# Expert blocks of an encoder layer: token rows through slot tables in DRAM instead of gather and scatter matmuls

## The reference

```python
def swiglu(x, w_gate, w_up, w_down):
    return (jax.nn.silu(x @ w_gate) * (x @ w_up)) @ w_down

logits = (xt @ w_router).astype(F32)
top_val, top_idx = lax.top_k(logits, TOP_K)          # TOP_K = 2 of 8
top_w = jax.nn.softmax(top_val, axis=-1)
...                                                  # slots grouped by expert into 128-row blocks
yp = lax.map(run, (xp.reshape(n_blocks, MOE_BLOCK, D), block_e)).reshape(P, D)   # run = swiglu
contrib = yp[dest] * w_s[:, None].astype(x.dtype)
out = jnp.zeros((T, D), x.dtype).at[tok_s].add(contrib)
```

## Time and profile before

| | |
|---|---|
| median of 3 runs | 1494.04 us (1493.0 to 1494.84) |
| span of the profiled execution | 1493.8 us |
| mixer 0, dense feed-forward, mixer 1 | 0 to 640 us |
| last mixer slabs, router, start of block 0 | 640 to 697 us |
| eight expert blocks, 98.45 us each | 692 to 1482 us |
| last scatter, additions, store | 1482 to 1493.8 us |
| busy: PE, DVE, ACT | 96%, 79%, 59% |

### The profile page before, as it was taken

One profiled execution on the slowest core, in us unless ns is written; L12 is line 12 of the kernel. 1 busy time (PEld: TensorE's weight loads), 2 busy tenths in 40 slices (PEclk: granted clock), 3 DMA queues, 4 the chain that ended last, 5 costly groups with the idle time before them and its releaser, 6 DMA issues.

```text
span 1493.8 us, 19784 instructions
## 1 busy us (share of the span) xinstructions
PE 1435.4 (96%) x6848; PEld 1177.4 (79%) x6848; DVE 1184.9 (79%) x1249; ACT 878.6 (59%) x944; POOL 40.9 (3%) x53
## 2 busy tenths in 40 slices
PE   6999898999999999888999999999999999999997
PEld 4887677788878876677888888888888888888786
DVE  5989875554459897746988989989898798898986
ACT  4345644434334456434777767777677677776774
POOL 0020001000000110100000000000000000000000
PEclk9999999999999999996999999999999999999999
DMA  7443224755244342332989979989799799897993
GB/s 285 174 174 141 85 87 154 271 190 195 92 169 170 141 151 104 134 113 100 385 296 360 386 281 387 353 296 393 280 370 387 273 396 339 318 387 279 374 385 110
DMA packets 56673, 372.06 MB, mean 249 GB/s; under 512 B 6706, under 2 KB 7278, under 8 KB 16570
## 3 DMA queue, kind: packets, MB, share of 16 engines
q1 hardware_dynamic: 55914, 368.82, 65.7%
q0 software_dynamic: 720, 2.72, 0.6%
HBM read 370.47 MB, written 1.05 MB: 249 GB/s over the span
## 4 chain that ended last, share of the span: by engine, by line
PE 82%; DVE 10%; issue 5%; ACT 2%; DVEq 0%; POOL 0%; DMA 0%; SPq 0%; POOLq 0%; ACTq 0%
PE bank L1536 19%; PE bank L1286 18%; PE bank L1287 17%; PE bank L1513 11%; PE bank L1333 5%; DVE w_lo L846 4%; PE bank L1299 3%; PE bank L1558 2%; PE bank L1328 2%; PE bank L1436 2%; PE bank L1423 1%; DVE ys L835 1%; DVE x L1194 1%; PE bank L1416 1%; ACT w_hi L570 1%
## 5 line engine op out<-in xcount | busy, mean ns | idle before, releaser
L846 DVE TENSOR_TENSOR w_lo<-raw,w_hi 128x2048 fp32r<-128x2048 f32 (+2 forms) x382 | 802.4, 2108 | 141.7 <-ACT w_hi L570 133.8
L570 ACT ACTIVATE w_hi<-raw 128x2048 fp32r<-128x2048 f32 (+2 forms) x382 | 674.0, 1769 | 179.8 <-PE bank L1536 97.6
L1286 PE MATMUL bank<-w_hi,hT_hi 128*128 128x512 f32 (+1 forms) x1232 | 492.1, 399 | 3.3 <-DVE act L1157 1.6
L1287 PE MATMUL bank<-w_hi,hT_lo 128*128 128x512 f32 (+1 forms) x1232 | 478.9, 389 | 0.0
L1286 PEld LDWEIGHTS bank<-w_hi,hT_hi 128*128 128x128 f32 x1232 | 233.0, 189 | 52.5 <-issue 5.5
L1287 PEld LDWEIGHTS bank<-w_hi,hT_lo 128*128 128x128 f32 x1232 | 233.3, 189 | 43.5 <-issue 1.0
L1513 PE MATMUL bank<-w_lo,hT_hi 128*128 128x512 f32 (+1 forms) x880 | 231.2, 385 | 0.0
L1513 PEld LDWEIGHTS bank<-w_lo,hT_hi 128*128 128x128 f32 x880 | 164.6, 188 | 31.6 <-DVE w_lo L846 0.3
L749 ACT ACTIVATE act_hi<-bank 128x256 fp32r<-128x256 f32 (+1 forms) x99 | 40.4, 408 | 138.5 <-PE bank L1299 138.5
L1536 PE MATMUL bank<-w_hi,act_lo 128*128 128x512 f32 (+1 forms) x440 | 118.7, 392 | 1.8 <-DVE act_lo L1163 1.8
L1536 PE MATMUL bank<-w_hi,act_hi 128*128 128x512 f32 (+1 forms) x440 | 119.0, 393 | 0.8 <-ACT act_hi L749 0.8
(11 more groups left out here) (212 smaller groups left out, 1115.6 us busy)
## 6 DMA issues: line engine op xcount, KB each, us to landing
raw<-in_moe SPq DMA_DIRECT2D x224, 1024.0 KB, 7.0
raw<-in_mix SPq DMA_DIRECT2D x56, 1024.0 KB, 4.9
raw<-in_dense SPq DMA_DIRECT2D x28, 1024.0 KB, 4.8
raw<-in_moe SPq DMA_DIRECT2D x42, 512.0 KB, 3.5
raw<-in_moe SPq DMA_DIRECT2D x16, 768.0 KB, 5.9
raw<-in_dense SPq DMA_DIRECT2D x5, 512.0 KB, 3.3
raw<-in_moe SPq DMA_DIRECT2D x8, 256.0 KB, 3.4
raw<-in_dense SPq DMA_DIRECT2D x2, 768.0 KB, 4.3
```

Source lines behind the costliest of these rows:

```text
L570: nc.scalar.activation(HI[:, split_slot, 0:width], RAW[:, raw_slot, 0:width], ACT.Copy)\
L846: vec.tensor_tensor(LO[:, split_slot, 0:width], RAW[:, raw_slot, 0:width], HI[:, split_slot, 0:width].bitcast(F32), ALU.subtract).then_inc ...
L1286: mm(out_, left[0], right[0], start=start, stop=False)
L1287: mm(out_, left[1], right[1], start=False, stop=False)
```

## The change

Two tables in DRAM are added, `slot_h` and `slot_y`, of 13 slots of 128 rows of 1024 floats. `slot_h` and the last four slots of `slot_y` are filled with zeros early in layer 0's feed-forward part, by two DMAs that ACT issues from a zeroed piece of `x_squared`. The router computes for each token and each of its two experts a row number (`rowi`), and POOL writes the normalized rows of all tokens to `slot_h` by four indirect DMAs of 128 rows. ACT loads the 128 rows of block 0 to `tok`; for all later blocks SP loads them, in the middle of the block before. PE transposes `tok` with eight transposes instead of the gather's 32 matmuls, ACT copies the result to `hT_hi`, and DVE subtracts for `hT_lo`. On the way back ACT and DVE each copy one bank of 512 columns to `y`, unscaled, and SP stores `y` to `slot_y` in the middle of the next block. After the last block POOL fetches each token's two result rows by four indirect DMAs, and DVE multiplies them with the token's weights and adds them to `x`. `psel`, `pselT`, `hg_hi`, `hg_lo`, `y_hi`, `y_lo` and all their matmuls and additions are gone. The order of the slabs is as before.

```diff
-    def router(dve, v, tt, ts, stt, gather_lo):
+    def router(dve, v, tt, ts, stt):
...
+        tt(place[:, :, :], counted, per_token(base), ALU.add)
+        ts(far[:, :, :], counted, float(CAP), None, ALU.is_ge, None, *drain_of(1, "pos", 0))
...
+        tt(chosen[:, 0, :, :], place[:, :, :], sel1[:, :, :], ALU.mult)
+        tt(chosen[:, 1, :, :], place[:, :, :], sel2[:, :, :], ALU.mult)
+        v.settle()
+        reduce(flat(R["rowf"][:, :, :]), chosen[:, :, :, :].rearrange("p k t e -> p (k t) e"))
+        v.settle()
+        v.do(vec.tensor_copy(R["rowi"][:, :, :], R["rowf"][:, :, :]), sem("rows_known"), 1)
...
@@ SP, block_slabs, between slabs 27 and 28
+                if b is not None:
+                    sp.wait_ge(tok_turned, 2 * b + 2)
+                    sp.dma_start(R["tok"][0:CAP, :], slot_h[bass.ds(sp.snap(CAP * b + 2 * CAP), CAP), :])\
+                        .then_inc(tok_loaded, 16)
+                    sp.wait_ge(y_taken, 2 * b + 2)
+                    sp.dma_start(slot_y[bass.ds(sp.snap(CAP * b), CAP), :], R["y"][0:CAP, :]).then_inc(y_free, 16)
...
@@ SP, the end
-        sp.wait_ge(scatter_added, 4 * nb + 4)
-        sp.dma_start(out.rearrange("(p t) d -> p t d", t=TB), X[:, :, :]).then_inc(sem("stored"), 16)
+        sp.wait_ge(y_taken, 2 * nb + 2)
+        sp.dma_start(slot_y[bass.ds(sp.snap(CAP * nb), CAP), :], R["y"][0:CAP, :]).then_inc(sem("last_y_stored"), 16)
+        out_rows = out.rearrange("(p t) d -> p t d", t=TB)
+        for tb in range(TB):
+            sp.wait_ge(sem("combined"), tb + 1)
+            sp.dma_start(out_rows[:, tb, :], X[:, tb, :]).then_inc(sem("stored"), 16)
...
@@ POOL
+        pool.wait_ge(y_free, 32)
+        pool.wait_ge(sem("h_scaled"), TB)
+        pool.wait_ge(sem("rows_known"), 1)
+        for k in range(TOPK):
+            for tb in range(TB):
+                pool.indirect_dma_start(slot_h, bass.IndirectOffsetOnAxis(R["rowi"][:, k, tb:tb + 1], 0), HG[:, tb, :], None)\
+                    .then_inc(sem("slots_filled"), 16)
+        pool.wait_ge(sem("last_y_stored"), 16)
+        for tb in range(TB):
+            for k in range(TOPK):
+                pool.indirect_dma_start(R["got"][:, k, tb, :], None, slot_y,
+                                        bass.IndirectOffsetOnAxis(R["rowi"][:, k, tb:tb + 1], 0))\
+                    .then_inc(sem(f"got{k}_{tb}"), 16)
...
@@ ACT
+                act.wait_ge(sem("zeros_ready"), 1)
+                act.dma_start(slot_h.rearrange("(b p) d -> p b d", p=P),
+                              X_SQUARED[:, 0, :].unsqueeze(1).broadcast_to([P, SLOT_ROWS // P, D])).then_inc(y_free, 16)
...
-                copy(R["hg_hi"][:, :, :], HG, sem("hg_hi_ready"), 1)
+                act.wait_ge(sem("slots_filled"), 16 * TOPK * TB)
+                act.dma_start(R["tok"][0:CAP, :], slot_h[CAP:2 * CAP, :]).then_inc(tok_loaded, 16)
...
+            def take_y(b):
+                act.wait_ge(slab_used, FFN_SLABS * b + first)
+                act.wait_ge(y_free, 16 * b + 32)
+                nc.scalar.activation(R["y"][0:CAP, 0:512], PS[4][0:CAP, :], ACT.Copy).then_inc(y_taken, 1)
...
@@ DVE
+            def turned_tokens_lo(b):
+                for i in range(2):
+                    dve.wait_ge(g_hi_ready, 2 * b + i + 1)
+                    vec.tensor_tensor(HTL[:, 4 * i:4 * i + 4, 0:CAP],
+                                      PS[6 + i][:, 0:4 * CAP].rearrange("p (k t) -> p k t", k=4),
+                                      HTH[:, 4 * i:4 * i + 4, 0:CAP].bitcast(F32), ALU.subtract).then_inc(g_lo_ready, 1)
...
+                take_y(nb)
+                for tb in range(TB):
+                    for k in range(TOPK):
+                        dve.wait_ge(sem(f"got{k}_{tb}"), 16)
+                        v.settle()
+                        stt(X[:, tb, :], R["got"][:, k, tb, :], R["tv"][:, 5 + k, tb:tb + 1], X[:, tb, :],
+                            ALU.mult, ALU.add, *((sem("combined"), tb + 1) if k else (None, None)))
...
@@ PE
+            def turn_tokens(b):
+                pe.wait_ge(tok_loaded, 16 * b + 16)
+                for i in range(2):
                     for k in range(4):
+                        kd = 4 * i + k
+                        ins = nc.tensor.transpose(PS[6 + i][:, k * CAP:(k + 1) * CAP],
+                                                  R["tok"][0:CAP, kd * P:(kd + 1) * P], IDENT[0:CAP, 0:CAP])
+                    ins.then_inc(tok_turned, 1)
```

More of the change, by code:

```diff
@@ L236, in trunk @@
                                    [("xv", [P, 3, TB, HW], F32)],
-                                   [("y_hi", [P, D], F32R), ("y_lo", [P, D], F32R),
-                                    ("psel", [P, TB, P], F32R), ("pselT", [P, TB, P], F32R)]]))
+                                   [("y", [P, D], F32), ("tok", [P, D], F32)]]))
     R.update(region("r_qkv", 3072, [[("wf3", [FH, 2048], F32), ("hyb", [1, 1024], F32)],
@@ L362, in router @@
         wait_filled(dve, 1, "pos", 0)
-        stt(flat(posm[:, :, :]), bank("pos", 0)[:, 0:TB * NE], 1.0, flat(sel[:, :, :]), ALU.add, ALU.mult)
-        ts(over[:, :], bank("pos", 0)[:, TB * NE:(TB + 1) * NE], float(P), None, ALU.is_gt, None,
-           *drain_of(1, "pos", 0))
+        counted = bank("pos", 0)[:, 0:TB * NE].rearrange("p (t e) -> p t e", t=TB)
+        ts(over[:, :], bank("pos", 0)[:, TB * NE:(TB + 1) * NE], float(CAP), None, ALU.is_gt)
+        tt(place[:, :, :], counted, per_token(base), ALU.add)
@@ L366, in router @@
+        ts(far[:, :, :], counted, float(CAP), None, ALU.is_ge, None, *drain_of(1, "pos", 0))
         v.settle()
-        ts(posm[:, :, :], posm[:, :, :], -1.0, None, ALU.add)
+        tt(cmp[:, 0, :, :], over[:, :].unsqueeze(1).broadcast_to([P, NE, NE]), tril, ALU.mult)
         reduce(nbf[:, 0:1], over[:, :])
         v.settle()
-        for tb in range(TB):
-            ts(R["psel"][:, tb, :], R["moec"][:, 0:P], posm[:, tb, 0:1], None, ALU.is_equal, None,
-               *((psel_ready, 1) if tb == 1 else (None, None)))
+        reduce(cnt[:, :], cmp[:, 0, :, :])
@@ new lines, in router @@
+        tt(place[:, :, :], place[:, :, :], far[:, :, :], ALU.add)
+        v.settle()
+        tt(chosen[:, 0, :, :], place[:, :, :], sel1[:, :, :], ALU.mult)
+        tt(chosen[:, 1, :, :], place[:, :, :], sel2[:, :, :], ALU.mult)
+        v.settle()
+        reduce(flat(R["rowf"][:, :, :]), chosen[:, :, :, :].rearrange("p k t e -> p (k t) e"))
+        v.settle()
+        v.do(vec.tensor_copy(R["rowi"][:, :, :], R["rowf"][:, :, :]), sem("rows_known"), 1)
+        for j in range(XTRA):
+            stt(oh[:, j, :], cnt[:, :], float(j), over[:, :], ALU.is_equal, ALU.mult)
@@ L387, in router @@
         tt(tv[:, 6, :], tv[:, 3, :], tv[:, 5, :], ALU.mult)
[L388 to L422, removed]
     def load_hidden(eng, layer):
@@ L824, in _ @@
                     ffn_block(b, True)
-                scaled_y_hi(FFN_SLABS * nb + first)
+                take_y(nb)
     @block.vector
@@ L1627, in _ @@
             else:
-                pe.wait_ge(psel_ready, 1)
-                for half in range(2):
-                    mm(PS[4 + half][:, :], R["pselT"][:, 0, :], HTH[:, 2 * half:2 * half + 2, :].rearrange("p a b -> p (a b)"),
-                       start=True, stop=True)
-                gather(0)
+                turn_tokens(0)
                 pe.wait_ge(sem("blocks_known"), 1)
@@ L1637, in _ @@
                     ffn_block(b, True)
-                scatter(nb)
     ctx.close()
```

209 lines of the change are left out of this document (74 added, 135 removed).

## The result

The kernel after takes 1470.87 us (median of four runs, 1469.01 to 1472.15) against 1494.44 us before on the same chip: a ratio of 0.9836, 95% interval 0.9823 to 0.985, so 1.6% faster. 1471 us were forecast. The span of the profiled execution is 1467.0 us, its own time 1469.01: in every run on record the time is the span and about 2 us. By that, the span of 1493.8 us of before belongs to an execution of some 1495.8 us, which is slower than the three runs that stood beside it ahead of the prediction.

A forecast was written before the change was run, and what follows sets the result against it. PE's matmul stream was taken to bound the expert blocks, with DVE and DMA close behind. Blocks -38.0, start +8.0, end +6.3 and zeros +0.5 sum to -23.2 us, giving 1471 us, range 1460 to 1488.

The forecast's parts named there:

- The total: Whole kernel: -38.0 + 8.0 + 6.3 + 0.5 = -23.2 us from a span of 1493.8, so 1471 us.
- PE's saving, 5.24 us a block, less 0.55: Expert blocks: gather 2.64, scatter 1.82, small matmuls 0.78 us saved; seven boundaries lose 0.55 each; 38.0 us in all.
- the laid-out waits: Block boundary: PE waits 0.3 us for tokens, 0.3 for slab 4's `w_lo`, 0.5 for the first `act_lo`.
- PE's stream sets the pace, so removed matmuls come back: Inside blocks: PE busy 98.20 of 98.45 us, so removed matmuls save their time, less new waiting at the boundaries.
- Rival 3: Block edges: ACT's and DVE's splits keep PE waiting, only half the saving remains, 1490 us; chance 0.06.
- DMA in the block, nothing: Inside blocks: added `tok` and `y` traffic, 1.05 MB or 2.7 us, fits and costs nothing; bound 21.6 us over eight blocks.
- the 4 us less 2.7: Slab loads inside a block: some 4 us to spare before ACT needs them, and 2.7 us of added transfers fit.
- Start, +8.0: Ahead of block 0: row numbers, four indirect DMAs, landing, `tok` load and transposes add 8.0 us; bounds +4.3 to +24.5.
- End, +6.3: Behind block 7: 17.7 us instead of 11.4 for store, four fetches, multiply-add and output; bounds +2.3 to +23.2.
- Zeros, +0.5: Dense slabs at about 254 us: 8.9 MB of zero fills cost two ACT issues, 0.5 us; bounds 0 to +25.
- same within 1 us up to 640 us: Trace ahead of the expert blocks: up to 640 us it should look the same within 1 us.
- The other signs: Blocks of about 93.7 us, PE over 98% busy; some 18 us at start and end; POOL issues about 1.2 us.

The follow-up runs named there:

- one execution of another kernel: The kernel after with ScalarE and VectorE taking the next block's turned tokens ahead of its first slab's split: 1480.32 us, block period 93.18 us.

## Why the prediction was right, point by point

- **The total.** -23.2 us were forecast, -26.8 is the difference of the two spans, -23.6 that of the medians. The remark that span and median differ by 0.2 us set two different executions side by side: a run's time is its span plus 2 us, and the profiled execution of before was one of the slower ones. The three stretches that the change touches sum to -25.3 us on the spans, so the terms together were 2.1 us short; the other 1.5 us of the -26.8 lie ahead of the router. That 1471 meets the median of after to 0.1 us is luck.
- **PE's saving, 5.24 us a block, less 0.55.** The size held (5.13 measured against 4.7, 40.8 in all against 38.0). The deduction was too large: the laid-out waits are there (0.54, 0.29, 0.39 us), but on the weight loads, which run ahead, and the wait for the first `act_lo`, which cost PE 0.41 us in before, costs 0.13. In all PE waits 1.47 us a block, against 1.53 before (table above).
- **Its mechanism held only in part.** The step "PE's stream sets the pace, so removed matmuls come back" counts PE alone. Without the matmuls but with VectorE's part of the scatter 2.89 of 4.9 us came back, and 4.00 without that part too. The sentence in the prediction that VectorE loses 4 us of work there named the condition; it was not given its price. Rival 3, by which half comes back, is near to right for a change that removes only the matmuls. The last 1.1 us up to the 5.13 are almost all waits that after does not have, and which of its other edits removes them is open.
- **DMA in the block, nothing.** Right, and with more room than the 4 us less 2.7 that were worked out: another 1 MB was free. The Trainium skill's limit in DMA: Bandwidth & Descriptors (Specifications), about 358 GB/s, is passed by the 398 GB/s over 94 us of the kernel with five extra stores, so it is no ceiling for this kernel.
- **Start, +8.0.** Measured +8.3. The row numbers were ready 2.4 us behind the counts as forecast. From the first issue to the last landing are 8.2 us (692.48 - 684.28) against 4.8 + 3.5: the landing of 4.2 us counts from the start of its issue, where the sum had put 3.5 behind the end. The load of `tok` took 3.35 us against 3.5, the steps from there to block 0 3.45 against 3.7. GpSimd's start 0.93 us behind `rowi` had been left out, and most of it was made up by these.
- **End, +6.3.** Measured +7.2. Missed were VectorE's needless split ahead of the copy of `y` (0.9 us) and landings of 5.4 instead of 3.5; against it the store of `y` took 2.9 us instead of 3.5, the output 3.05 instead of 3.3, and a fetch's landing counts from the start of its issue, where the sum had put it behind the end (about 1 us).
- **Zeros, +0.5.** Not measurable in after, but for another reason than the one given. The step looked at DMA bandwidth and the slabs' lead; what counts is how long ScalarE stands in the issue. The margin was what PE had still to do while ScalarE stood for 4.13 us, and one execution of another kernel went beyond it.
- **The sign "same within 1 us up to 640 us".** It failed by a little: after is 1.5 us ahead there, 1.1 of it ahead of everything that was changed. The other signs came as said: blocks of 93.33 us with PE busy throughout, no wait for `raw`, some 18 us at either end.

## What to carry to other kernels

A removed matmul is worth its full time only if nothing else then comes late. Here VectorE was busy for 87 of 98 us, and the gather's matmuls gave 81% back, the scatter's 22%, until the vector work beside them went too: cut each alone, and read the block's period. A round trip through DRAM cost nothing here between blocks that follow each other, where the DMA engines had time to spare, and 7 to 8 us ahead of the first and behind the last; keeping the matmul path for the first block won 9.3 us. Beware of a second large fill on an engine that has work to do behind it; putting the fills on another engine was not run.

## What the runs showed of the hardware

- An indirect DMA of 128 rows of 4 KB costs GpSimd 0.94 to 1.13 us, one per 1.29 us in a row, and lands 4.2 us (write) to 5.4 us (read) after the start of its issue.
- A DMA issue takes 0.4 us of ScalarE's queue, but behind a fill of 6.7 MB 5.9 us, in one execution 14.3, and behind one of 13.3 MB 31.2 us.
- Matmuls of 512 columns start 0.227 us apart while nothing is missing, of 128 columns 0.108 us. A wait of 0.3 to 0.5 us on the weight load of one cost PE 0.03 to 0.27 us.
- After PE had waited 7.8 us, its granted clock was 0.50 when it began again at 265.0 us, and 1.00 from about 271 us on; after a wait of 24.7 us it was 0.50 at 282.1 us and 1.00 from about 285 us on. At 0.50 matmuls of 512 columns start 0.43 us apart.
